# A drain after each piece of GpSimd's weight subtractions, in a two-block transformer kernel on one core

## The chip, the core and the metric

The kernel runs on one core of one Trainium2 chip. A core has five engines that take their own instruction streams and meet at semaphores: TensorE (PE in the rows, its weight loads PEld), VectorE (DVE), ScalarE (ACT), GpSimd (POOL) and SyncE (SP), which here issues the loads of weights. The metric is the device time of one execution in microseconds; the median of several runs is compared.

## The reference

Two transformer blocks follow each other on one sequence of 256 tokens with 1024 channels, all in float32.

```python
def reference(x, ...):
    x = first_block(x, ...)      # adaLN; retention + 3 groups of dilated attention, gated; squared-ReLU MLP (4096)
    return second_block(x, ...)  # 2 layers: MLA + mLSTM + SSD mixers, layernorm; hierarchical MoE, 16 experts of 256

proj = h @ w_in                                   # first block, 1024 x 12800
x = x + g2 * (jnp.square(jax.nn.relu(h @ w1)) @ w2)
h = jax.nn.silu(jnp.einsum('bsd,edf->bsef', x, w_gate)) * jnp.einsum('bsd,edf->bsef', x, w_up)
h = h * combine[..., None]                        # every expert is computed, weights are zero for most
return jnp.einsum('bsef,efd->bsd', h, w_down)
```

Nearly all of the time goes into products of the 256 tokens with weight matrices.

## The kernel before

The weights come as one stream of **units** of 128 partitions by 1024 columns, 448 of them through the engines in the same way (six rounds of eight more, for the modulation, go to VectorE alone). A float32 product is made of three products of rounded numbers: each operand is split into a high part (rounded, `_hi`) and the rest (`_lo`), and TensorE adds hi x hi, hi x lo and lo x hi (L923 to L925, helper `mm3`). A unit takes 12 matmuls of 512 columns: two token tiles, two halves, three products.

For each unit, in the order of the stream:

- SyncE loads two units at a time into `w_raw`, a ring of eight (L465). Before it overwrites a pair it waits for `lo_ready`.
- ScalarE writes the rounded copy into `w_hi`, a ring of four slots (L549, `hi`), once the data has landed and once TensorE has given the slot's former unit back (`unit_used`). It then increments `hi_ready`.
- GpSimd computes `w_lo = w_raw - w_hi` (L511, `lo`) once `hi_ready` has come, in pieces of `width` columns: two of 512 in the first block and for the experts, four of 256 in the front half of each layer of the second block. The last piece increments `lo_ready`.
- TensorE waits for `lo_ready`, multiplies, and increments `unit_used`.

The order is written out by hand, and each engine works through its list strictly. GpSimd does little else: 32 small products for the SSD mixer (L532) in each layer's middle and a few memsets. VectorE computes norms, rotations, softmax sums and the lo parts of the activations (L1505, L1513), multiplies the ada weights (L1583), squares the MLP's activations (L1846), weighs the experts' (L2209). It works on float32 and puts a `drain` between dependent operations of its own (`dep = dve.drain`).

The stages in order of the stream: retention inputs (units 0 to 47), first attention input, retention output, other attention inputs, gates, outputs (up to unit 127), the MLP (64 units, eight tiles), and then twice a layer of 128 units: inputs, MLA, mLSTM and SSD, output (31 units), router (1), experts (96, six for each).

Of the kernel before, what the change touches and what calls it, by code (L numbers as in the profile page):

```python
# [58 lines left out]
UNIT = 1024  # L59
# [116 lines left out]
def program(nc, A):  # L176

    ctx = ExitStack()
    with ctx:
# [272 lines left out]
        def spans(d):  # L452

            return ((0, 0, S), (1, P, S)) if d == 0 else ((0, 0, P), (1, 0, S))
# [7 lines left out]
        def _(sp):  # L462
# [15 lines left out]
            for (_, kind, k), (at, _, _) in zip(rounds, rounds[1:]):  # L478
                for s in range(n_ring):
                    used = k * RAW + PIECE * (s + 1)  # L480
                    sp.wait_ge(ada_used if kind == "ada" else lo_ready, used)
                    piece(at * n_ring + s, s)
                    if at == 1 and s == 1:
                        sp.dma_start(x_sb[:, :, :], A["x"].rearrange("b (t p) d -> p (b t) d", p=P)).then_inc(x_loaded, 16)
                        sp.dma_start(W[:, 0:D], A["norm1_g"].partition_broadcast(P)).then_inc(norm1_loaded, 16)
                if at == 1:
                    sp.dma_start(ident[:, :], A["identity"]).then_inc(ident_loaded, 16)
                if at == 2:
                    sp.dma_start(arena[:, 18432:20480], A["const1"]).then_inc(cst_loaded, 16)
                    sp.dma_start(inv_row, A["inv_freq"].partition_broadcast(P)).then_inc(pos_loaded, 16)  # L490
                    sp.dma_start(pos_i[:, :], A["pos_col"]).then_inc(pos_loaded, 16)
# [11 lines left out]
        @block.gpsimd  # L503
        def _(pool):
            pool.memset(mod[:, 2 * D:], 0.0).then_inc(mod_cleared_b, 1)
            def lo(n, k, width):

                pool.wait_ge(hi_ready, n + (k + 1))  # L508
                for a in range(0, UNIT, width):
                    cols = slice(a, a + width)  # L510
                    i = pool.tensor_tensor(w_lo[:, k % SLOTS, cols], w_raw[:, k % RAW, cols],  # L511
                                           w_hi[:, k % SLOTS, cols].bitcast(F32), ALU.subtract)
                i.then_inc(lo_ready, 1)

            def lo_round(n, width):
                for s in range(RAW):
                    lo(n, s, width)

            with pool.Fori(0, U_LAYERS // RAW) as i:
                lo_round(i * RAW, UNIT // 2)  # L520
            ahead = L_OUT + SLOTS
            with pool.Fori(0, LAYERS) as l:
                n = l * L_UNITS + U_LAYERS
                with pool.Fori(0, ahead // RAW) as i:
                    lo_round(i * RAW + n, UNIT // 4)
                for k in range(ahead // RAW * RAW, ahead):
                    lo(n, k, UNIT // 4)

                for j in range(2 * SH):
                    pool.wait_ge(sexp_ready, l * 8 + (j + 1))  # L530
                    for st, a, b in spans(j % 2):
                        i = pool.tensor_tensor(sw[:, j % 4, st, a:b], sw[:, j % 4, st, a:b], cbs[j // 4][:, st * S + a:st * S + b], ALU.mult)  # L532
                    i.then_inc(sw_ready, 1)
                for k in range(ahead, (ahead // RAW + 1) * RAW):
                    lo(n, k, UNIT // 4)
                with pool.Fori(ahead // RAW + 1, L_UNITS // RAW) as i:
                    lo_round(i * RAW + n, UNIT // 2)
# [1836 lines left out]
```

## Time and profile before

| | before |
|---|---|
| median of 3 runs | 1718.28 us (1718.05 to 1719.68) |
| the profiled execution's own time | 1714.52 us |
| its span in the trace | 1712.7 us, 20704 instructions |
| granted TensorE clock, mean | 0.941 |

The span is what the trace covers; the execution's own time lies 1.8 us above it. The profile is of one execution. Times in rows are microseconds from the span's start, or nanoseconds where it says so. Register, branch and drain instructions have no rows of their own in these views. A group of several instructions in the timeline ("x2") has the start of the first and the time to the end of the last.

### The profile page before, as it was taken

What the parts mean: (1) busy time and instruction counts of PE and PEld (TensorE: products, weight loads), DVE (VectorE), ACT (ScalarE), POOL (GpSimd) and SP (SyncE); (2) the same over time, 40 slices, a digit from 0 to 9 for tenths busy, and PEclk for the clock granted to TensorE, in tenths of its full rate; (3) what the DMA queues carried; (4) which work ended last, traced back from release to release, by engine and by line L of the source; (5) the groups of instructions that cost most, each with busy time, mean ns of one, the idle gap of its engine ahead of it and who ended that gap; (6) DMA issues with size and microseconds to landing.
All of it is one profiled execution on the core that took longest, in us unless ns stands there. A gap on an engine that the chain in (4) does not pass through costs nothing.

```text
span 1712.7 us, 20704 instructions
## 1 busy us (share of the span) xinstructions
PE 1516.0 (89%) x6848; PEld 1221.3 (71%) x6848; DVE 649.9 (38%) x1092; ACT 716.5 (42%) x1049; POOL 1231.9 (72%) x1061
## 2 busy tenths in 40 slices
PE   6979799999777999887787899999778778999996
PEld 2767577888665888676666688888667656888885
DVE  7666924222545111456745100010467463000003
ACT  4322444445433444344443444444344433444442
POOL 3887797877573999685226799999575355999994
PEclk8989999999897999998898899999889888999998
DMA  9665667444432555353103454555442023555551
GB/s 386 246 231 188 252 225 264 172 148 148 160 131 98 196 174 193 123 200 112 58 1 116 167 196 175 192 190 180 156 147 91 25 87 122 188 182 194 184 184 50
DMA packets 44043, 279.72 MB, mean 163 GB/s; under 512 B 5405, under 2 KB 8605, under 8 KB 11582
## 3 DMA queue, kind: packets, MB, share of 16 engines
q1 hardware_dynamic: 37138, 263.82, 42.7%
q10 hardware_dynamic: 6830, 14.92, 2.4%
q8 instruction: 44, 0.72, 0.2%
q14 instruction: 31, 0.25, 0.0%
HBM read 274.53 MB, written 4.19 MB: 163 GB/s over the span
## 4 chain that ended last, share of the span: by engine, by line
POOL 50%; issue 31%; PE 16%; DVE 1%; POOLq 1%; DVEq 0%; ACT 0%; ACTq 0%
POOL w_lo L511 49%; PE G L923 3%; PE G L924 3%; PE G L925 3%; PE AC L923 2%; PE AC L925 2%; PE AC L924 2%; POOL arena L532 1%; PE T L1006 0%; POOLq L508 0%; DVE x_sb L1858 0%; DVE x_sb L1856 0%; DVE sm L1915 0%; DVE x_sb L1878 0%; PE T L962 0%
## 5 line engine op out<-in xcount | busy, mean ns | idle before, releaser
L511 POOL TENSOR_TENSOR w_lo<-w_raw,w_hi 128x512 fp32r<-128x512 f32 (+1 forms) x1024 | 1210.4, 1211 | 446.4 <-ACT w_hi L549 446.2
L549 ACT ACTIVATE w_hi<-w_raw 128x1024 fp32r<-128x1024 f32 x448 | 471.9, 1059 | 641.2 <-PE G L925 355.9
L923 PE MATMUL G<-w_hi,xT_hi 128*128 128x512 f32 x944 | 391.4, 415 | 34.0 <-POOL w_lo L511 22.9
L924 PE MATMUL G<-w_lo,xT_hi 128*128 128x512 f32 x944 | 379.2, 402 | 0.0
L925 PE MATMUL G<-w_hi,xT_lo 128*128 128x512 f32 x944 | 378.6, 401 | 0.0
L923 PEld LDWEIGHTS G<-w_hi,xT_hi 128*128 128x128 f32 x944 | 185.2, 196 | 78.9 <-issue 19.8
L923 PE MATMUL AC<-w_hi,yT_hi 128*128 128x512 f32 x576 | 229.6, 399 | 6.6 <-DVE yT_lo L1505 4.4
L924 PE MATMUL AC<-w_lo,yT_hi 128*128 128x512 f32 x576 | 226.5, 393 | 0.0
L925 PE MATMUL AC<-w_hi,yT_lo 128*128 128x512 f32 x576 | 226.3, 393 | 0.0
L925 PEld LDWEIGHTS G<-w_hi,xT_lo 128*128 128x128 f32 x944 | 184.1, 195 | 40.9
L924 PEld LDWEIGHTS G<-w_lo,xT_hi 128*128 128x128 f32 x944 | 185.2, 196 | 36.0
L2209 DVE SCALAR_TENSOR_TENSOR arena<-arena,sm,G 128x256 f32<-128x256 f32 x64 | 27.9, 478 | 335.3 <-ACT arena L592 335.3
L1505 DVE TENSOR_TENSOR yT_lo<-T,yT_hi 128x256 fp32r<-128x256 f32 (+2 forms) x128 | 53.9, 458 | 247.1 <-ACT yT_hi L561 246.8
L923 PEld LDWEIGHTS AC<-w_hi,yT_hi 128*128 128x128 f32 x576 | 110.7, 192 | 31.1 <-POOL w_lo L511 3.7
L925 PEld LDWEIGHTS AC<-w_hi,yT_lo 128*128 128x128 f32 x576 | 110.0, 191 | 23.3
L924 PEld LDWEIGHTS AC<-w_lo,yT_hi 128*128 128x128 f32 x576 | 110.5, 192 | 22.1
L923 PE MATMUL AC<-w_hi,xT_hi 128*128 128x512 f32 x256 | 106.1, 415 | 6.1 <-POOL w_lo L511 5.9
L925 PE MATMUL AC<-w_hi,xT_lo 128*128 128x512 f32 x256 | 100.6, 393 | 0.0
L924 PE MATMUL AC<-w_lo,xT_hi 128*128 128x512 f32 x256 | 100.6, 393 | 0.0
L1006 PE MATMUL T<-ident,arena 128*128 128x128 f32 x292 | 49.0, 301 | 47.7 <-DVE arena L2209 13.7
L1583 DVE SCALAR_TENSOR_TENSOR mod<-w_raw,sm,mod 128x1024 f32<-128x1024 f32 x48 | 76.0, 1584 | 18.0 <-DMA w_raw<-w_stream 14.8
L1006 PEld LDWEIGHTS T<-ident,arena 128*128 128x128 f32 x292 | 38.2, 154 | 61.7 <-issue 42.4
(366 smaller groups left out, 1402.7 us busy)
## 6 DMA issues: line engine op xcount, KB each, us to landing
w_raw<-w_stream SPq DMA_DIRECT2D x248, 1024.0 KB, 4.8
mod<-rows ACTq DMA_DIRECT2D x2, 2048.0 KB, 10.1
rel_scratch<-arena ACTq DMA_DIRECT2D x1, 3072.0 KB, 18.1
mod<-rows ACTq DMA_DIRECT2D x3, 476.0 KB, 3.7
x_sb<-x SPq DMA_DIRECT2D x1, 1024.0 KB, 9.4
arena<-const SPq DMA_DIRECT2D x1, 1024.0 KB, 9.6
mod<-gn_g ACTq DMA_DIRECT2D x1, 1024.0 KB, 6.6
arena<-gn_b ACTq DMA_DIRECT2D x1, 1024.0 KB, 8.7
```

Of the source, the lines that this page charges most:

```text
L511: i = pool.tensor_tensor(w_lo[:, k % SLOTS, cols], w_raw[:, k % RAW, cols], w_hi[:, k % SLOTS, cols].bitcast(F32), ALU.subtract)
L532: i = pool.tensor_tensor(sw[:, j % 4, st, a:b], sw[:, j % 4, st, a:b], cbs[j // 4][:, st * S + a:st * S + b], ALU.mult)
L549: act.activation(w_hi[:, k % SLOTS, :], w_raw[:, k % RAW, :], ACT.Copy).then_inc(hi_ready, 1)
L923: pe.matmul(out, xh, wh, start=start, stop=False)
L924: pe.matmul(out, xh, wl, start=False, stop=False)
L925: return pe.matmul(out, xl, wh, start=False, stop=stop)
L1006: i = pe.transpose(T[:, t, c * P:(c + 1) * P], src[:, t, c * P:(c + 1) * P], ident[:, :])
L1505: dve.tensor_tensor(dst_lo[:, c0:c0 + nch, s], T[:, t, 0:nch * P].rearrange("p (c n) -> p c n", n=P), dst_hi[:, c0:c0 + nch, s].bitcast(F3 ...
L1583: dve.scalar_tensor_tensor(m, w_raw[:, s, :], csil[:, s:s + 1], m, ALU.mult, ALU.add).then_inc(ada_used, 1)
L2209: i = dve.scalar_tensor_tensor(moe_h[:, t, :], ffn_a[:, t, :], comb[:, bass.ds(e0 + (t * EXPERTS + e), 1)], G[:, t, DE:2 * DE], ALU.mult, ...
```

## The change

`lo` gets a drain of GpSimd behind each piece: between two pieces of a unit, and behind the last piece of each unit, whose increment of `lo_ready` stays on the piece itself. This holds in all stages, for both widths. A drain makes the engine's sequencer wait until what it has issued is complete before it issues more.

```diff
@@ def lo(n, k, width)
                     i = pool.tensor_tensor(w_lo[:, k % SLOTS, cols], w_raw[:, k % RAW, cols],
                                            w_hi[:, k % SLOTS, cols].bitcast(F32), ALU.subtract)
+                    if a + width < UNIT:
+                        pool.drain()
                 i.then_inc(lo_ready, 1)
+                pool.drain()
```

No other instruction moves. On GpSimd this is the end of the loop over the first block's units, before the change (`w_lo`, `w_raw` and `w_hi` as above; L519 is the loop, L508 the wait in `lo`):

```order
L508 REGISTER_ALU
L511 TENSOR_TENSOR w_lo<-w_raw,w_hi 128x512 [waits hi_ready]
L511 TENSOR_TENSOR w_lo<-w_raw,w_hi 128x512
L519 REGISTER_ALU
L519 COMPARE_AND_BRANCH
```

The register instruction computes the value that the next unit's wait needs; it stands behind the last piece, and at a loop's end a branch stands there too. After the change the rows are the same with a drain behind each piece, so that these instructions come after a drain.

## Rows read from the trace of the kernel before

**Rows 1.** The page: busy us, share of the span, instructions.
```profile
PE 1516.0 (89%) x6848; PEld 1221.3 (71%) x6848; DVE 649.9 (38%) x1092; ACT 716.5 (42%) x1049; POOL 1231.9 (72%) x1061
```
**Rows 2.** Windows: length; PE, PEld, DVE, ACT, POOL busy; clock, DMA, GB/s.
```profile
237.00:500.00 263.00, 246.56 (x1163) 201.08 (x1163) 92.37 (x150) 121.97 (x189) 193.65 (x151) 0.97 0.51 179
717.00:770.00 53.00, 43.74 (x186) 34.05 (x184) 31.94 (x46) 24.88 (x40) 44.13 (x58) 0.90 0.44 159
955.00:1211.00 256.00, 254.88 (x1153) 210.75 (x1152) 26.27 (x62) 110.27 (x134) 224.13 (x176) 1.00 0.52 185
```
**Rows 3.** Timeline, second layer's experts: start, us, instruction, idle before.
```profile
1504.45 0.87 DVE L2209 SCALAR_TENSOR_TENSOR arena<-arena,sm,G 128x256 f32<-128x256 f32 x2 [10.94 <-ACT arena L592]
...
1521.25 0.87 DVE L2209 SCALAR_TENSOR_TENSOR arena<-arena,sm,G 128x256 f32<-128x256 f32 x2 [10.93 <-ACT arena L592]
...
1600.86 1.06 ACT L549 ACTIVATE w_hi<-w_raw 128x1024 fp32r<-128x1024 f32 x1 [1.66 <-PE G L925]
...
1602.00 2.55 POOL L511 TENSOR_TENSOR w_lo<-w_raw,w_hi 128x512 fp32r<-128x512 f32 x2 [0.17 <-ACT w_hi L549]
...
1603.24 1.30 POOL L511 TENSOR_TENSOR w_lo<-w_raw,w_hi 128x512 fp32r<-128x512 f32 x1
1603.38 0.39 PE L923 MATMUL AC<-w_hi,yT_hi 128*128 128x512 f32 x1
...
1606.10 0.39 PE L923 MATMUL AC<-w_hi,yT_hi 128*128 128x512 f32 x1
...
1609.15 0.19 PEld L923 LDWEIGHTS G<-w_hi,xT_hi 128*128 128x128 f32 x1
```
**Rows 4.** Groups of instructions by line and form, GpSimd.
```profile
L511 POOL TENSOR_TENSOR w_lo<-w_raw,w_hi 128x512 fp32r<-128x512 f32 x768 | 1021.6, 1357 | 261.0 <-ACT w_hi L549 260.8
L511 POOL TENSOR_TENSOR w_lo<-w_raw,w_hi 128x256 fp32r<-128x256 f32 x256 | 188.8, 775 | 185.4 <-ACT w_hi L549 185.4
```
**Rows 5.** The page: a costly group (busy us, mean ns), DMA issues (KB, landing us).
```profile
L2209 DVE SCALAR_TENSOR_TENSOR arena<-arena,sm,G 128x256 f32<-128x256 f32 x64 | 27.9, 478 | 335.3 <-ACT arena L592 335.3
...
w_raw<-w_stream SPq DMA_DIRECT2D x248, 1024.0 KB, 4.8
```
**Rows 6.** One line's instructions: ns min/median/max, first and last start, forms.
```profile
L511 POOL TENSOR_TENSOR w_lo<-w_raw,w_hi x1024: 713/1288/2350, 32.8 to 1690.0; 128x512 fp32r<-128x512 f32 x128, 128x256 fp32r<-128x256 f32 x43
...
L1583 DVE SCALAR_TENSOR_TENSOR mod<-w_raw,sm,mod x48: 1270/1285/2148, 6.7 to 278.2; 128x1024 f32<-128x1024 f32 x48
```
**Rows 7.** Timeline, VectorE, group norm of a retention head.
```profile
193.98 1.23 DVE L1669 TENSOR_TENSOR arena<-arena 128x1024 f32<-128x1024 f32 x1
195.28 1.23 DVE L1674 TENSOR_TENSOR arena<-arena 128x1024 f32<-128x1024 f32 x1
```
**Rows 8.** Timeline, MLP, VectorE and GpSimd.
```profile
582.26 1.50 DVE L1846 TENSOR_TENSOR arena<-arena 128x1024 f32<-128x1024 f32 x1 [10.91 <-ACT arena L590]
...
604.95 1.50 DVE L1846 TENSOR_TENSOR arena<-arena 128x1024 f32<-128x1024 f32 x1 [10.94 <-ACT arena L590]
...
604.08 3.52 POOL L511 TENSOR_TENSOR w_lo<-w_raw,w_hi 128x512 fp32r<-128x512 f32 x2 [0.17 <-ACT w_hi L549]
```
**Rows 9.** Waits from 717 to 770, then from 115 to 240: us, times, longest.
```profile
PEld G L923 <- POOL w_lo L511: 5.8, 4, 2.8
...
PE G L923 <- POOL w_lo L511: 8.9, 2, 7.4
```
**Rows 10.** Timeline, GpSimd, chains at a layer's start and before 250 us.
```profile
740.29 11.38 POOL L511 TENSOR_TENSOR w_lo<-w_raw,w_hi 128x256 fp32r<-128x256 f32 x16 [5.46 <-ACT w_hi L549]
752.33 22.24 POOL L511 TENSOR_TENSOR w_lo<-w_raw,w_hi 128x256 fp32r<-128x256 f32 x32 [0.66 <-ACT w_hi L549]
...
898.49 16.89 POOL L511 TENSOR_TENSOR w_lo<-w_raw,w_hi 128x256 fp32r<-128x256 f32 x22 [21.55 <-ACT w_hi L549]
...
213.81 35.36 POOL L511 TENSOR_TENSOR w_lo<-w_raw,w_hi 128x512 fp32r<-128x512 f32 x25
```
**Rows 11.** Timeline, GpSimd, from 58 us.
```profile
59.45 18.28 POOL L511 TENSOR_TENSOR w_lo<-w_raw,w_hi 128x512 fp32r<-128x512 f32 x11
```

## The prediction, made before the changed kernel was run

> **What bounds the kernel now.** I read the busy shares first, then windows by stage, then the order in time of the steady stages. TensorE is busy 89% of the span, GpSimd 72%, ScalarE 42%, VectorE 38% [rows 1]. The windows show two kinds of stage [rows 2]. Among the experts TensorE is busy 254.88 of 256.00 us at granted clock 1.00, its upper level, 2.4 GHz. At the start of a layer it is busy only 43.74 of 53.00 us, at 0.90.
>
> The steady order is in [rows 3]. TensorE begins a unit every 2.72 us (1603.38, 1606.10, then 1609.15 after four transposes). ScalarE rounds a unit in 1.06 us, as soon as TensorE has given a slot back. GpSimd starts 0.08 us after that (1600.86 + 1.06 = 1601.92, start 1602.00), needs 2.55 us for its two pieces, and stands idle 0.17 us. So GpSimd is nearly as slow as TensorE here: its idle 28% of the span is not one reserve, and in the steady stages it comes in crumbs of 0.17 us.
>
> What protects TensorE is a **lead**. The unit whose subtraction ends at 1604.55 is first used at 1609.15, 4.6 us later; the one at 1606.10 was ready already. A stage can thus lose about 4.5 us on GpSimd before TensorE notices, once, unless TensorE pauses for something else and the lead grows back. Where the lead is gone already, each lost nanosecond counts: at the first layer's start its weight load waits 5.8 us for L511, and before 240 us TensorE waits 8.9 us for it [rows 9].
>
> **What one drain costs.** The program holds 448 units: 384 with 768 pieces of 512 columns and 64 with 256 pieces of 256 [rows 4]. The change adds a drain behind each of the 1024 pieces. Nothing is removed, no DMA is added. Queued behind a drain are, on GpSimd, the next piece, and at a unit's end the register instruction and the next wait for hi_ready. The increment of lo_ready sits on the last piece, ahead of its drain, so a drain inside a unit delays that unit, and the one at its end only the next. Behind these wait TensorE (lo_ready) and SyncE, whose loads wait for lo_ready too; a load refills a slot needed eight units later (over 21 us) and lands in 4.8 us [rows 5], so that stays covered as long as that distance holds.
>
> The trace shows no drained GpSimd piece, so I bound it. Undrained, the second piece starts 1.24 us after the first (1602.00, 1603.24), whose kind lasts 1.288 us in the median [rows 3, 6]: they overlap by 0.05 us. A drain removes this overlap at least: 0.05 us is the lower bound. A GpSimd piece released by another engine's completion starts 0.08 us after it, as above; 0.05 + 0.08 = 0.13 us. VectorE has drains in this kernel: L1667, L1669 and L1674 have one between each two, and L1669 (193.98 + 1.23) is followed by L1674 at 195.28, 0.07 us later; two undrained L2209 take 0.87 us against 2 x 0.478, so they overlap by 0.09; the difference is 0.16 us [rows 5, 7]. I take **0.14 us**, between the two ways of reading it. At a unit's end the register instruction, which now runs while the piece is being computed, comes after the drain. No row shows its time. It is bounded by nothing and by the 0.08 us in which a whole wait is answered; I take 0.04. The register and branch instructions at a loop's end, once in eight units, are a few more of the kind: 0 to 0.6, I take 0.3, or 0.04 a unit.
>
> A unit of two pieces then costs 0.14 + 0.18 + 0.04 = **0.36 us** more, and a back-to-back unit goes from 2.50 (2.55 less the 0.05) to 2.86 us. A unit of four pieces costs 3 x 0.14 + 0.18 + 0.02 = **0.62 us** more.
>
> The Trainium skill (GPSIMD Engine Reference, section 3.1) puts the dispatch of one VectorE instruction at about 156 ns and says that GpSimd has two software hops where VectorE has one. An estimate from that page, 2 x 156 = 0.31 us a drain, would about double what I take, and the sum with it; the start after 0.08 us in this trace speaks against it.
>
> **Where it lands on the path.**
> - *Experts.* One expert is six units in 16.80 us (L2209 at 1504.45 and 1521.25 [rows 3]). Drained, GpSimd needs 6 x 2.86 = 17.16, so 0.36 too much; 16 experts make 5.8, less the lead of 4.5: 1.3 us a layer, **2.6 us**.
> - *MLP.* A tile of eight units takes 22.69 us (L1846 at 582.26 and 604.95); one piece of a tile is held up by that VectorE operation (3.52 against 2.55 us) [rows 3, 8]. Drained: 8 x 2.86 + 0.97, less 0.14 since the held-up piece was going to wait anyway, is 23.7: 1.0 too much, seven times, less at most 4.5 of lead. Between 2.5 and 7, I take **5 us**.
> - *Layer starts.* Here the units have four pieces, and GpSimd runs them without a gap: 16 pieces from 740.29, 32 in 22.24 us from 752.33 (2.78 a unit), 22 from 898.49 [rows 10], that is some 17 units a layer, with TensorE waiting for them [rows 9]. Some of them still fill slots before TensorE needs them; I count 13 of the 17: 13 x 0.62 = 8 us a layer, **16 us**. This is the largest term.
> - *First 300 us.* Again chains without a gap (25 pieces from 213.81 [rows 10]). Until about 240 us many pieces alternate with VectorE's operations of two inputs (11 pieces in 18.28 us, 1.66 each instead of 1.25 [rows 11]). A piece that stands waiting for VectorE loses nothing by starting 0.14 us later. I count the free ones: some 20 units x 0.36 = **7 us**.
> - *Attention inputs and gates, and the rest of each layer.* From 237 to 500 us GpSimd is busy 193.65 of 263.00 us [rows 2]: idle for a quarter, and with the lead that covers 0.36 us in each unit of some 3.5: nothing. Without that cover the 60-odd units there would cost 0.36 each, 22 us.
>
> Sum: 2.6 + 5 + 16 + 7 = 30.6 us. Made against the profiled execution (span 1712.7, its time 1714.52) that is 1745.1 us. The median of the runs is 1718.28, 3.8 us above the profiled one, so I forecast 1718.3 + 30.6, **1749 us**.
>
> Ends: with 0.05 us a drain and nothing for registers, a unit of two costs 0.10 and one of four 0.20. MLP and experts stay under TensorE's time (8 x 2.60 + 0.97 = 21.8), and 26 x 0.20 + 20 x 0.10 = 7 us remain: 1725. With 0.16 a drain and 0.13 for registers at every unit's end, a unit of two costs 0.45, of four 0.77. MLP: 8 x 2.95 + 0.8 = 24.4, 1.7 x 7 - 4.5 = 7; experts 2 x (16 x 0.9 - 4.5) = 20; layer starts 26 x 0.77 = 20; first stretch 9; together 56: 1774.
>
> **Rivals.**
> 1. *No change:* the drain ends with the piece, and the 0.17 us of idle take in all that is left. For it: those gaps. Against it: the chains without a gap, with TensorE waiting behind them; it needs a drain under 0.02 us, below the overlap that is surely lost. Time 1718.
> 2. *Faster, by the port that GpSimd and VectorE share.* Operations of VectorE are held up by L511's pieces: L1583, 48 times before 280 us, lasts 1285 ns in the median and up to 2148 [rows 6]. If the pause after each piece lets such operations through, each gains up to 0.86 us; with half of the 48 held up that is 20 us at most. At my price of a drain it does not pay for the 30.6; with the drain at 0.05 (7 us) it decides from 9 such waits on, and all 24 gone give 1718 + 7 - 20 = 1705. Against it: in the alternating stretch the two engines already take turns after every single piece [rows 11], and a pause of 0.1 us in 1.4 meets an operation 1 time in 14, under 2 us in all. The Trainium skill (SBUF — State Buffer, "SBUF: two separate sides") calls the shared pair an exclusive lock that is held for the whole instruction; the trace agrees, with waits of 0.86 us.
> 3. *A dear drain.* A unit takes 2.78 us in four pieces and 2.50 in two [rows 3, 10], so each piece has a fixed part of 0.14 us. If a queued piece hides most of a larger one, and an emptied engine shows it again, a drain costs 0.13 + 0.14 = 0.27 us, with registers 0.6 a unit of two (3.1 us) and 1.14 a unit of four: MLP 8 x 3.1 + 0.9 = 25.7, 3 x 7 - 4.5 = 16; experts 2 x (16 x 1.8 - 4.5) = 49; layer starts 26 x 1.14 = 30; first 12: 107 us, 1825. For it: a drain has to empty the engine, which no row shows. Against it: both nearest gaps are 0.07 and 0.08.
>
> **Chances.** Forecast, a drain of 0.05 to 0.17 us: 0.78. No change: 0.05. Faster: 0.04. Dear: 0.13. The range runs from 1720 to 1780: it takes in my two ends and reaches down into the no-change case, and leaves out the faster and the dear one. A measurement of this kernel can tell about 0.2%, 3.4 us. Faster 0.04, same 0.05, slower 0.91.
>
> **What the profile after should show.** In the experts GpSimd's two pieces taking 2.70 to 2.75 us instead of 2.55 and lying 2.82 to 2.88 us apart, its waits for L549 gone there late in the stage, TensorE waiting for L511 in small steps, an expert lasting 17.0 to 17.2 us near its end. At the layers' starts a unit of four pieces in 3.4 instead of 2.79 us. VectorE's and ScalarE's own durations as before. The prediction is wrong if the pieces themselves get longer, if the clock shows more stretches at its lower level, 1.2 GHz, because TensorE pauses (from 717 to 770 us the clock is 0.90 with TensorE busy 83% of the time; from 237 to 500 it is 0.97 at 94% [rows 2]), or if VectorE's held-up operations become fewer.

## The result and the profile after

The changed kernel takes 1794.51 us in the median, the kernel before 1718.16 in the same comparison: 1.0455 of it, 95% interval 1.0428 to 1.0482. The forecast of slower was right, but 1749 was not, and 1794.5 lies above the range: 76 us were added where 30.6 were predicted. The profiled execution took 1793.63 us, span 1791.8. Medians here and below are of executions that agree: one of the four of E2 took 3806 us and is left out of its median.

The page of the changed kernel: a group (busy us, mean ns, idle before it and what ended it), then the chain that ended last.

```profile
POOLq 68%; issue 27%; PE 3%; POOL 1%; DVE 0%; DVEq 0%; ACT 0%
...
L511 POOL TENSOR_TENSOR w_lo<-w_raw,w_hi 128x512 fp32r<-128x512 f32 (+1 forms) x1024 | 1227.1, 1198 | 501.5 <-ACT w_hi L552 327.4
```

The pieces are no longer than before (mean 1198 ns; the page of before has 1211). The time went into the gaps behind them: the chain that ended last runs now through GpSimd's queue (POOLq, 68%, nearly all of it at the two drains' lines, L514 and L516); in the page of before it had GpSimd's pieces for 50% and TensorE for 16%. In the waits of GpSimd, 92.5 us in 365 places wait for nothing that the profile shows:

```profile
POOL w_lo L511 <- ACT w_hi L552: 327.4, 85, 28.5
POOL w_lo L511 <- issue: 92.5, 365, 0.6
```

Timeline of the changed kernel among the second layer's experts, the place of [rows 3]:

```profile
1642.48 0.87 DVE L2212 SCALAR_TENSOR_TENSOR arena<-arena,sm,G 128x256 f32<-128x256 f32 x2 [11.67 <-ACT arena L595]
...
1660.17 0.87 DVE L2212 SCALAR_TENSOR_TENSOR arena<-arena,sm,G 128x256 f32<-128x256 f32 x2 [11.37 <-ACT arena L595]
...
1678.17 0.87 DVE L2212 SCALAR_TENSOR_TENSOR arena<-arena,sm,G 128x256 f32<-128x256 f32 x2 [11.37 <-ACT arena L595]
...
1649.70 2.73 POOL L511 TENSOR_TENSOR w_lo<-w_raw,w_hi 128x512 fp32r<-128x512 f32 x2 [0.22 <-issue]
1652.48 0.19 PEld L926 LDWEIGHTS G<-w_hi,xT_hi 128*128 128x128 f32 x1 [0.33 <-POOL w_lo L511]
1652.65 2.73 POOL L511 TENSOR_TENSOR w_lo<-w_raw,w_hi 128x512 fp32r<-128x512 f32 x2 [0.22 <-issue]
1655.42 0.19 PEld L926 LDWEIGHTS G<-w_hi,xT_hi 128*128 128x128 f32 x1 [0.36 <-POOL w_lo L511]
1655.90 2.73 POOL L511 TENSOR_TENSOR w_lo<-w_raw,w_hi 128x512 fp32r<-128x512 f32 x2 [0.53 <-issue]
```

The reader sees all the prices here. Two pieces take 2.73 us instead of 2.55: the second now starts 0.14 us after the first one's end instead of 0.04 to 0.05 before it, so the drain between them costs about 0.19. Behind a unit there are 0.22 us of gap instead of an overlap of 0.04, so the second drain with the register instruction costs 0.26, and a loop's end has a gap of 0.53, 0.31 more. Units lie 2.95 us apart. TensorE waits for L511 in both units that the rows show, and an expert takes 18.00 us (1660.17 to 1678.17) instead of 16.80. At a layer's start, the place of [rows 10]:

```profile
759.92 3.37 POOL L511 TENSOR_TENSOR w_lo<-w_raw,w_hi 128x256 fp32r<-128x256 f32 x4 [4.66 <-ACT w_hi L552]
763.51 3.35 POOL L511 TENSOR_TENSOR w_lo<-w_raw,w_hi 128x256 fp32r<-128x256 f32 x4 [0.22 <-issue]
```

A unit of four pieces takes 3.59 us instead of 2.78, 0.81 more. In the MLP, the place of [rows 8], a tile takes 24.58 us instead of 22.69:

```profile
636.75 2.13 DVE L1849 TENSOR_TENSOR arena<-arena 128x1024 f32<-128x1024 f32 x1 [10.93 <-ACT arena L593]
...
661.33 2.12 DVE L1849 TENSOR_TENSOR arena<-arena 128x1024 f32<-128x1024 f32 x1 [10.97 <-ACT arena L593]
```

**Stage by stage.** TensorE executes the same 6848 weight loads in each of the kernels here, so the start of the same load in two traces compares them place by place. The table gives the length of a stretch in the profiled execution of the kernel before, and what each kernel adds to it; in brackets the microseconds in which the clock was granted at its lower level, 1.2 GHz.

| stretch of before, us | length | after | E1 mid | E2 end | E3 wide | E4 narrow |
|---|---|---|---|---|---|---|
| 7 to 272, first stretch | 265.6 (34) | +10.1 (34) | +1.1 (34) | +8.4 (20) | +10.2 (34) | +1.5 (17) |
| 272 to 564 | 291.1 (38) | -3.0 (34) | -1.9 (34) | -2.6 (34) | -2.7 (34) | 0.0 (38) |
| 564 to 722, MLP | 158.2 (0) | +10.6 (4) | 0.0 (0) | +1.8 (0) | +10.8 (4) | 0.0 (0) |
| 722 to 857, layer 1 | 134.9 (38) | +4.9 (40) | +3.5 (38) | +0.7 (38) | -4.8 (26) | +2.5 (27) |
| 857 to 898, SSD and mLSTM | 41.9 (7) | +10.4 (34) | +10.1 (31) | +10.2 (34) | +1.6 (14) | +10.7 (34) |
| 898 to 962 | 63.1 (20) | +2.9 (20) | +3.3 (20) | +0.5 (14) | -2.5 (14) | +1.1 (14) |
| 962 to 1220, experts | 258.4 (6) | +11.8 (4) | 0.0 (6) | 0.0 (3) | +12.9 (5) | 0.0 (3) |
| 1220 to 1239, layer 2 starts | 19.2 (4) | +3.8 (3) | +4.1 (8) | +2.2 (7) | 0.0 (5) | +5.3 (11) |
| 1239 to 1341, layer 2 | 102.1 (17) | +3.2 (19) | +5.9 (27) | +0.4 (17) | +0.7 (17) | +6.6 (27) |
| 1341 to 1377, SSD and mLSTM | 35.8 (7) | +9.4 (29) | +10.4 (31) | +10.0 (31) | +0.1 (7) | +10.9 (31) |
| 1377 to 1445 | 67.6 (20) | +2.5 (20) | +3.4 (27) | +3.2 (27) | -0.4 (20) | +3.7 (24) |
| 1445 to 1700, experts | 255.0 (0) | +11.9 (0) | 0.0 (0) | 0.0 (0) | +13.0 (0) | 0.0 (0) |

Two stretches stand out that the prediction had at nothing: the SSD and mLSTM part of each layer, 10.4 and 9.4 us, each with over 20 us more at the lower clock. GpSimd has almost no weights to subtract there (one unit of four pieces; the other 16 of its 20 instructions in the rows below are products for the SSD mixer). Windows over this part, of the kernel before and then of the changed one (length; PE, PEld, DVE, ACT, POOL busy; clock, DMA, GB/s):

```profile
857.00:898.00 41.00, 33.23 (x196) 27.77 (x196) 20.26 (x49) 17.58 (x45) 12.15 (x20) 0.92 0.00 1
```
```profile
880.00:931.00 51.00, 45.45 (x196) 38.85 (x195) 19.81 (x47) 16.96 (x45) 12.07 (x20) 0.67 0.00 1
```

The same 196 matmuls, at clock 0.67 instead of 0.92, take 45.45 us of TensorE instead of 33.23.

The short stretch from 1220 to 1239 is the start of the second layer. Weight loads wait there for GpSimd's pieces, in the kernel before (1220 to 1240) and in the changed one (1268 to 1292):

```profile
PEld G L923 <- POOL w_lo L511: 5.8, 3, 3.4
```
```profile
PEld G L926 <- POOL w_lo L511: 10.2, 4, 4.1
```

### The profile page after: what moved, and what is told of

It is laid out like the page before. It is cut to its first block, busy times and chain, and to the rows that moved or that the text cites. A ratio compares the mean times of both kernels' runs of the same rounds, so it can differ in the third digit from the quotient of the medians.

```text
span 1791.8 us, 21728 instructions
## 1 busy us (share of the span) xinstructions
PE 1577.8 (88%) x6848; PEld 1235.8 (69%) x6848; DVE 637.4 (36%) x1092; ACT 716.6 (40%) x1049; POOL 1248.6 (70%) x1061
## 4 chain that ended last, share of the span: by engine, by line
POOLq 68%; issue 27%; PE 3%; POOL 1%; DVE 0%; DVEq 0%; ACT 0%
POOLq L514 36%; POOLq L516 31%; POOL arena L535 1%; POOLq L508 1%; PE AC L926 1%; PE AC L927 0%; PE G L926 0%; PE AC L928 0%; PE G L928 0%; PE G L927 0%; POOLq L539 0%; POOL w_lo L511 0%; POOLq L522 0%; DVE x_sb L1859 0%; DVEq L1536 0%
## 5 line engine op out<-in xcount | busy, mean ns | idle before, releaser
L511 POOL TENSOR_TENSOR w_lo<-w_raw,w_hi 128x512 fp32r<-128x512 f32 (+1 forms) x1024 | 1227.1, 1198 | 501.5 <-ACT w_hi L552 327.4
L926 PE MATMUL G<-w_hi,xT_hi 128*128 128x512 f32 x944 | 396.0, 420 | 45.6 <-POOL w_lo L511 32.4
L926 PE MATMUL AC<-w_hi,yT_hi 128*128 128x512 f32 x576 | 240.0, 417 | 20.7 <-POOL w_lo L511 16.3
L926 PE MATMUL AC<-w_hi,xT_hi 128*128 128x512 f32 x256 | 108.2, 422 | 10.9 <-POOL w_lo L511 10.8
L1586 DVE SCALAR_TENSOR_TENSOR mod<-w_raw,sm,mod 128x1024 f32<-128x1024 f32 x48 | 79.8, 1662 | 20.8 <-DMA w_raw<-w_stream 17.5
L1009 PE MATMUL T<-ident,arena 128*128 128x128 f32 x292 | 49.2, 302 | 42.1 <-DVE arena L2212 11.8
## 6 DMA issues: line engine op xcount, KB each, us to landing
mod<-rows ACTq DMA_DIRECT2D x2, 2048.0 KB, 10.1
```

What stands on the lines that cost most here:

```text
L926: pe.matmul(out, xh, wh, start=start, stop=False)
L1009: i = pe.transpose(T[:, t, c * P:(c + 1) * P], src[:, t, c * P:(c + 1) * P], ident[:, :])
L1586: dve.scalar_tensor_tensor(m, w_raw[:, s, :], csil[:, s:s + 1], m, ALU.mult, ALU.add).then_inc(ada_used, 1)
```

## The experiments

### Which of the two drains, and in which units

E1, drains between the pieces only:

```diff
                     if a + width < UNIT:
                         pool.drain()
                 i.then_inc(lo_ready, 1)
-                pool.drain()
```


> Only the drains between the pieces of a unit (576 of the 1024); none behind the last piece. The trace of the changed kernel shows the next piece 0.14 us after a drained one's end instead of 0.04 before it: 0.19 us each. Theory A (a pipeline with a lead: a unit's time counts only where GpSimd becomes slower than TensorE or the lead is gone): a unit of two pieces takes 2.69 us, under TensorE's 2.80 among the experts and 2.84 in the MLP, so both stages cost nothing; the layers' starts (0.56 a unit) and the first 300 us cost 20 us, 1738. Rival B (each drain costs its share of the 76 us wherever it stands, 75 ns each): 43 us, 1761. If the clock's longer lower stretch in the mLSTM and SSD part comes back with these drains, 20 us more on A: 1758, and the windows there tell it.

E2, the drain behind the unit only:

```diff
-                    if a + width < UNIT:
-                        pool.drain()
                 i.then_inc(lo_ready, 1)
                 pool.drain()
```


> Only the drain behind the last piece of each unit (448 of the 1024). The trace of the changed kernel shows the next unit 0.22 us after the last piece's end instead of 0.04 before: 0.27 us each, 0.57 at a loop's end. Theory A: a unit of two pieces takes 2.77 us and one in eight 3.08, 2.81 in the mean: about TensorE's pace, so MLP and experts cost under 5 us; all together 15 us, 1733. Rival B (75 ns a drain): 33 us, 1751. A and this run's sum with the one without end drains would give 35 of 76 us: the rest arises only when both stand together. With the clock's part 20 us more.

E3, both, in units of two pieces only (E4 the same with `UNIT // 4`):

```diff
-                    if a + width < UNIT:
+                    if a + width < UNIT and width == UNIT // 2:
                         pool.drain()
                 i.then_inc(lo_ready, 1)
-                pool.drain()
+                if width == UNIT // 2:
+                    pool.drain()
```


> Both kinds of drain, but only in units of two pieces of 512 columns (first block, MLP, experts); the layers' starts as before. Theory A with the measured prices: first 300 us 10, MLP 12, experts 2 x 12, together 47 us, 1765, and the mLSTM and SSD part without a longer stretch at the lower clock. Rival B: 768 drains of 75 ns, 57 us, 1775.

> Both kinds of drain, but only in units of four pieces of 256 columns (the front of each layer of the second block). Theory A: 10 to 12 us a layer while TensorE waits for GpSimd at the layer's start and at the output projection, 24 us, 1742; and if the long stretch at the lower clock in the mLSTM and SSD part is set off by these delays, 20 us more, 1762. Rival B: 256 drains of 75 ns, 19 us, 1737, with the clock as before. With the run of the wide units alone the two sums should add up to 76 us: theory A says the stages are independent.

| | median, us | ratio, 95% interval |
|---|---|---|
| kernel before (with E1 to E4) | 1719.5 | |
| E1, 576 drains | 1754.3 | 1.0184, 1.0124 to 1.0245 |
| E2, 448 drains (three executions) | 1745.24 | 1.0140, 1.0064 to 1.0215 |
| E3, 768 drains | 1756.3 | 1.0210, 1.0150 to 1.0269 |
| E4, 256 drains | 1755.87 | 1.0199, 1.0140 to 1.0258 |

The medians alone decide nothing: E1 lies between theory A's 1738 and its 1758 with the clock, E2 between A's 1733 and the 1751 of 75 ns a drain, to which A with the clock's part (1753) comes close. The stretches decide. In the MLP and the experts of the two layers E1 adds 0.0, 0.0 and 0.0, E2 1.8, 0.0 and 0.0, both together (E3) 10.8, 12.9 and 13.0. A price per drain cannot give that: the 256 drains of either kind there would have to cost the same alone as together. The timelines show why. GpSimd among the experts, first E1, then E2:

```profile
1499.20 2.73 POOL L511 TENSOR_TENSOR w_lo<-w_raw,w_hi 128x512 fp32r<-128x512 f32 x2
1502.39 16.35 POOL L511 TENSOR_TENSOR w_lo<-w_raw,w_hi 128x512 fp32r<-128x512 f32 x12 [0.47 <-ACT w_hi L551]
1519.21 1.28 POOL L511 TENSOR_TENSOR w_lo<-w_raw,w_hi 128x512 fp32r<-128x512 f32 x1 [0.47 <-ACT w_hi L551]
```
```profile
1559.28 2.55 POOL L511 TENSOR_TENSOR w_lo<-w_raw,w_hi 128x512 fp32r<-128x512 f32 x2 [0.22 <-issue]
1562.05 2.55 POOL L511 TENSOR_TENSOR w_lo<-w_raw,w_hi 128x512 fp32r<-128x512 f32 x2 [0.22 <-issue]
1564.91 2.55 POOL L511 TENSOR_TENSOR w_lo<-w_raw,w_hi 128x512 fp32r<-128x512 f32 x2 [0.31 <-issue]
1567.67 2.54 POOL L511 TENSOR_TENSOR w_lo<-w_raw,w_hi 128x512 fp32r<-128x512 f32 x2 [0.22 <-issue]
1570.84 2.54 POOL L511 TENSOR_TENSOR w_lo<-w_raw,w_hi 128x512 fp32r<-128x512 f32 x2 [0.62 <-issue]
```

E1 runs six units in 16.35 us and then still waits 0.47 us for ScalarE: six fit into an expert's 16.80. E2 uses 2.77 us for most units and 22.6 us for eight with the loop's end, where TensorE needs 22.4: over the 96 units that is some 2.4 us, and the lead of 4.6 takes it in. Both together need 3.00 us a unit with the loop's end. So E3 gives theory A its 10.8 in the MLP (12 expected) and 13 us a layer in the experts (12), and 1756.3 instead of 1765 since the stretches at 272 to 564 and 722 to 857 gave back 7.5 us, most of it with less time at the lower clock.

The other half: in all runs with drains in the narrow units (E1, E2, E4) the SSD and mLSTM part takes 10 to 11 us more a layer, with 31 or 34 us at the lower clock; in E3 it takes 1.6 and 0.1. E4's 1755.87 comes nearer to the 1762 that was expected with the clock's part than to the 1742 without it or to the 1737 of 75 ns a drain. E3 and E4 add up to 37 + 36 = 73 of the 76 us.

### What sends the clock down

In each layer GpSimd's program has three units (12 pieces) right before the products for the SSD mixer, on which TensorE waits. E5 drains these three alone; E6 is the changed kernel without these; E7 has no drain, but the last of the three in eight pieces of 128 columns.

```diff
 # E5 (E6: the reverse); drained is an argument of lo() that guards both drains
                 for k in range(ahead // RAW * RAW, ahead):
-                    lo(n, k, UNIT // 4)
+                    lo(n, k, UNIT // 4, True)
```


> Drains, of both kinds, only in the three units of each layer that stand right before the SSD products on GpSimd (12 drains a layer, 24 in all); everything else as before. In the runs with drains in the layers' front the stretch from the first of these products to the end of that part took 10 to 11 us longer a layer, beside 20 us more at the lower clock, and it did not where only the wide units had drains. Theory C: a delay of well under 1 us on GpSimd's way to the products makes TensorE's pause fall so that the clock goes to its lower level for some 27 us instead of 3: this kernel then takes 2 x 10 us more for 24 drains, 1738. Rival D: it takes the sum of delays from the whole front of a layer: then this kernel is at 1719 to 1721 and shows the clock as before. At 75 ns a drain it would be 2 us.

> The changed kernel without the drains in those three units of each layer, 1000 of the 1024 drains. Theory C: the long stretch at the lower clock goes, and with it 20 us: 1775. Rival D: 1793, as the changed kernel.

```diff
 # E7, from the kernel before
                 for k in range(ahead // RAW * RAW, ahead):
-                    lo(n, k, UNIT // 4)
+                    lo(n, k, UNIT // 8 if k == ahead - 1 else UNIT // 4)
```


> The kernel before, without any drain, but the last unit before the SSD products is subtracted in eight pieces of 128 columns instead of four of 256. A piece has a fixed part of about 0.14 us, so the unit ends 0.5 to 0.6 us later, like a unit with drains. Theory C: if it is the delay and not the drain that sends the clock down, this kernel shows the same 10 us a layer, 1738. Rival E, that a drain does something of its own there: 1719 with the clock as before.

| | median, us | ratio, 95% interval | SSD and mLSTM part, two layers, us added |
|---|---|---|---|
| kernel before (with E5 to E8) | 1717.92 | | |
| E5, 24 drains | 1738.52 | 1.0104, 1.0043 to 1.0165 | 12.0, 9.2 |
| E6, 1000 drains | 1782.77 | 1.0360, 1.0298 to 1.0422 | 9.8, 8.6 |
| E7, no drain | 1734.29 | 1.0089, 1.0064 to 1.0114 | 10.3, 9.4 |

By the medians 24 drains cost 20.6 us, a quarter of what 1024 do, and a kernel without any drain, whose last unit merely ends later, costs 16.4. The kernel before scatters in this comparison (1713.8 to 1733.75), which makes the intervals wide; both lie above 1. GpSimd before the products, in the kernel before and in E7:

```profile
858.59 3.26 POOL L511 TENSOR_TENSOR w_lo<-w_raw,w_hi 128x256 fp32r<-128x256 f32 x4 [20.01 <-ACT w_hi L549]
861.81 4.45 POOL L532 TENSOR_TENSOR arena<-arena,scr 128x256 f32<-128x256 f32 x8
```
```profile
859.99 3.82 POOL L511 TENSOR_TENSOR w_lo<-w_raw,w_hi 128x128 fp32r<-128x128 f32 x8 [20.13 <-ACT w_hi L549]
863.78 4.42 POOL L532 TENSOR_TENSOR arena<-arena,scr 128x256 f32<-128x256 f32 x8
```

and the windows over the part in E7:

```profile
857.00:909.00 52.00, 44.87 (x198) 38.57 (x199) 19.64 (x47) 17.59 (x47) 12.68 (x24) 0.70 0.00 1
```

The unit takes 3.82 instead of 3.26 us, 0.56 longer, and the clock is 0.70, near the 0.67 after the change. It is thus the delay, not the drain (against rival E), and a delay of 0.6 us is enough (against rival D). In the kernel before, the clock stays at its upper level for 27 us from 852 on and then falls for 3.4 us (6.8 in the second layer). In both layers of the changed kernel and of E1, E2, E4, E5 and E7 it falls after 13.7 us and stays down for 27 to 31 us; in E3 it stays up for 27 us as before. Windows in the first layer, one of before and two of the changed kernel:

```profile
852.00:879.50 27.50, 25.13 (x177) 21.71 (x175) 9.12 (x27) 14.09 (x40) 12.15 (x20) 0.99 0.01 1
```
```profile
875.00:889.00 14.00, 12.30 (x76) 9.88 (x75) 6.76 (x19) 7.93 (x21) 6.55 (x11) 0.98 0.00 1
889.50:920.00 30.50, 30.00 (x118) 26.80 (x119) 5.84 (x18) 11.03 (x27) 5.02 (x9) 0.50 0.00 1
```

TensorE had pauses before it fell (12.30 us busy of 14.00), and by the profile, which models the matmuls' ends, hardly any while the clock stayed down (30.00 of 30.50). Which of the pauses decides, and why the clock does not come back sooner, no run here shows. The kernel before can take the slower course too, it seems: one of its 13 executions in this comparison took 1733.75 us at a mean clock of 0.925, where the other twelve have 0.933 to 0.946. It has no trace. E6 speaks against the narrow form of theory C: its profiled execution, at 1793.73, has both long stretches although the three units are undrained, while its other four runs took 1779.98 to 1782.94 us, at mean clocks of 0.935 to 0.937 against 0.929. So these units are enough to set it off but not the only ones that can, and the time differs from run to run. That the four faster runs lack one of the two stretches fits their 11 us, but no trace of theirs shows it, and the mean clock does not tell it surely: two executions of the changed kernel at 1794.5 us have 0.932 and 0.935.

### The price of one more drain

E8, every drain twice:

```diff
                     if a + width < UNIT:
                         pool.drain()
+                        pool.drain()
                 i.then_inc(lo_ready, 1)
                 pool.drain()
+                pool.drain()
```


> Each of the 1024 drains twice. The second finds an idle engine, so it costs only what the sequencer needs for one more such instruction: between the end of a drain and the start of the next instruction the trace of the changed kernel has 0.07 us, so about 0.08 us each. Theory A (a lead that is already used up, so all of it counts in the stages where GpSimd sets the pace): a tile of the MLP 16 x 0.08 = 1.3 us, an expert 12 x 0.08 = 1.0, the layers' starts 26 x 0.32 = 8, the first 300 us 3: together 9 + 31 + 8 + 3 = 51 us over the changed kernel, 1845. If a drain's price were the emptying of the engine alone, the second would be free: 1794.

1840.68 us, 1.0701 (1.0637 to 1.0765): 46 us over the changed kernel, 51 expected, where a free second drain would have left it at 1794. GpSimd among the experts:

```profile
1769.11 1.29 POOL L511 TENSOR_TENSOR w_lo<-w_raw,w_hi 128x512 fp32r<-128x512 f32 x1 [0.21 <-issue]
1770.69 1.29 POOL L511 TENSOR_TENSOR w_lo<-w_raw,w_hi 128x512 fp32r<-128x512 f32 x1 [0.29 <-issue]
1772.19 1.29 POOL L511 TENSOR_TENSOR w_lo<-w_raw,w_hi 128x512 fp32r<-128x512 f32 x1 [0.21 <-issue]
```

The gaps are 0.21 and 0.29 us where the changed kernel has 0.14 and 0.22: 0.07 for a second drain, which has nothing to wait for. It is not free, so a drain's price is not the emptying alone. The drains' own records, which these views leave out, divide the 0.19 us of a first drain in the changed kernel: 0.05 is the overlap that is lost, 0.05 passes from the piece's end to the drain's, and 0.09 from there to the next piece's start (medians of 574 places).

### Making room under the threshold, and wider pieces

E9 is the changed kernel with the wide units in one piece, E10 the same without drains (the edit for the first block and the MLP; the experts have the same):

```diff
-                lo_round(i * RAW, UNIT // 2)
+                lo_round(i * RAW, UNIT)
```


> The changed kernel, but the units of the first block, the MLP and the experts are subtracted in one piece of 1024 columns instead of two of 512, so that a wide unit has one drain, behind it. A piece's fixed part is 0.14 us: a unit takes 2.36 + 0.27 + 0.04 = 2.67 us, under the 2.80 of TensorE among the experts and the 2.84 in the MLP. Theory A (threshold): MLP and experts are back at the times of the kernel before in spite of a drain in every unit; what is left is the layers' fronts with their clock stretch (the run with the narrow units alone: 36 us) and 3 us before 300 us: 1757. Rival B (a drain costs 75 ns wherever it stands): 448 - 64 + 256 = 640 drains, 48 us, 1766. Rival F: a piece twice as long holds up VectorE's operations longer (up to 2.4 us instead of 1.2): another 5 to 10 us in the first 300 us and in the MLP.

> No drains; the wide units in one piece of 1024 columns. Where GpSimd sets the pace (chains without a gap in the first 300 us) 0.14 us a unit are saved, 3 us; elsewhere TensorE sets it: 1715. Rival F, the longer hold on VectorE, would put it at 1720 to 1730.

E9 takes 1775.86 us (1.0362, 1.0329 to 1.0394), not 1757; E10 1743.57 (1.0150, 1.0121 to 1.0180), not 1715. As a total E9 is nearer to the 1766 of 75 ns a drain; the stretches separate the two questions. Against the kernel before, E9 adds 0.0 us in the MLP and 0.0 in the experts of either layer: with a drain behind each of the 256 units, nothing. GpSimd there:

```profile
1563.16 2.41 POOL L511 TENSOR_TENSOR w_lo<-w_raw,w_hi 128x1024 fp32r<-128x1024 f32 x1 [0.33 <-ACT w_hi L552]
1565.88 2.39 POOL L511 TENSOR_TENSOR w_lo<-w_raw,w_hi 128x1024 fp32r<-128x1024 f32 x1 [0.31 <-ACT w_hi L552]
```

2.39 us and a gap of 0.22 fit under 2.72, and it waits for ScalarE again. That is theory A at its plainest. In the first 272 us E9 and E10 lose 16.4 and 12.8 us, more than rival F said; E9 also has 58 us at the lower clock there, against 34 in the kernel before and 31 in E10. VectorE in E10, in a rotation:

```profile
63.85 2.89 DVE L1631 TENSOR_TENSOR arena<-arena 128x512 f32<-128x512 f32 x1
66.81 2.74 DVE L1633 TENSOR_TENSOR arena<-arena 128x512 f32<-128x512 f32 x1
69.47 2.89 DVE L1634 TENSOR_TENSOR arena<-arena 128x512 f32<-128x512 f32 x1
```

GpSimd does eight pieces in 21.47 us around them, 2.68 each, so the two engines take turns. The same operations last 1.62 to 1.78 us in the kernel before, beside pieces half as long, and 0.68 to 0.69 where nothing holds them up. E10 has a long clock stretch in the second layer besides (8.9 us added), without a drain and with the last unit hardly longer (3.38 us against 3.26), so a shift of another origin can set it off too.

E11 and E12 go the other way in the layers' fronts, without drains: E11 takes two pieces of 512 instead of four of 256 in all the units there, E12 only in the three before the SSD products.

```diff
 # E12; E11 has the same edit in the other two places of the front
                 for k in range(ahead // RAW * RAW, ahead):
-                    lo(n, k, UNIT // 4)
+                    lo(n, k, UNIT // 2)
```


> No drains; the units in the front of each layer in two pieces of 512 instead of four of 256. 0.28 us less a unit on some 13 units a layer for which TensorE waits: 7 us saved, 1711. Rival F: VectorE's small operations there wait up to 1.2 us instead of 0.7 for each piece: slower, 1720 to 1730. The clock's stretch after the SSD products need not change, since the units before them end earlier, not later.

> No drains; only the three units right before the SSD products in two pieces of 512. They end up to 0.8 us earlier. Theory C says that these units' end decides over the clock's long stretch: earlier is safe, so 1717 to 1718, and none of the runs at 1724 to 1734 that the kernel before shows now and then. If the clock depends on the place of the pause in both directions, it may as well show the long stretch: 1738.

E11 takes 1712.78 us against 1717.39 of before: 0.9980, 0.9965 to 0.9994, faster by a little than the kernel before, where 1711 was expected. It saves 7.0 us from 722 to 857, and gives part back in the second layer. E12 takes 1721.84, 1.0020 (1.0004 to 1.0036), neither the 1717 to 1718 nor the 1738 expected. Its last unit before the products takes 2.96 us instead of 3.26. No stretch of 27 us at the lower clock appears, but an earlier end is not free either: there are 17 us at the lower level in the first layer's SSD part instead of 7, which adds 2.8 us, and 30 instead of 17 from 1239 to 1341, which adds 4.7.

## Why the prediction was wrong

- **The mechanism behind the four terms of the sum was right.** GpSimd stops hiding behind TensorE where it becomes slower than it, or where the lead is gone. E1, E2, E3 and E9 show the threshold from both sides. The changed kernel's experts and MLP tiles, at 18.00 and 24.58 us, are what the units give: 6 x 2.95 + 0.31 for the loop's end, and 8 x 2.95 + 0.31 + 0.69 for the piece that the VectorE operation holds up.
- **The step that failed first is the price of a drain.** I took 0.14 us and 0.18 at a unit's end with the registers, "between the two ways of reading it". Measured: 0.19 and 0.26. The start 0.08 us after another engine's completion, on which the 0.13 rested, is not the start behind a drain: that comes 0.14 us after the piece's end, and E8 puts 0.07 us on one more drain alone. VectorE's 0.16 was nearer. A unit of two so costs 0.19 + 0.26 + 0.04 = 0.49 us instead of 0.36, a third more than I took. Since the cost counts above a threshold, the terms grew by far more: an expert has 1.2 us over TensorE's time instead of 0.36, so the experts' 2.6 us became 23.7 (11.8 and 11.9 a layer), and the MLP's 5 became 10.6.
- **The step that failed second is "the rest of each layer: nothing".** 19.8 us came from the SSD and mLSTM parts, where the products begin some 0.6 us later a layer by the drains themselves (3.61 + 0.23 us from the last unit's start, instead of 3.26 less an overlap of 0.04), and nearly all of the rest goes with the lower clock. The prediction named the clock as something that would make it wrong, in the wrong place: it looked for it where TensorE would wait for L511, and it came in a part whose pauses are there anyway, after a delay of 0.6 us.
- **Layers' starts, 16 us, came out near, by luck in part:** 17.3 us in the five stretches around them. The price was too low and the count too high: at 0.81 us instead of 0.62, 17.3 us are 21 units in both layers instead of 26.
- **First 300 us:** 7 forecast, 10.1 less 3.0 in the next stretch measured. The count of 20 free units at the new price of 0.49 gives 9.8, near the 10.1. No run confirms the count: E1 adds 1.1 there and E2 8.4 at another share of lower clock.
- **Rivals.** No change and faster are excluded. VectorE's held-up operations did not become fewer: L1583, now L1586, has a mean of 1662 ns instead of 1584, and the squaring in the MLP takes 2.13 us instead of 1.50. The dear drain, given 0.13, was 0.27 us with 1825 us as its sum. The measured price lies between the two: a unit of two costs 0.49 us, against my 0.36 and the 0.60 of this rival, and the experts 23.7 against my 2.6 and its 49. In total the rival was off by 31 us and I by 46. The estimate of 0.31 us a drain from the Trainium skill (GPSIMD Engine Reference, section 3.1) was too high by the trace's 0.19 and 0.26. At that price the sum would not have doubled either, as I wrote, but more than tripled: the rival with 0.27 us a drain comes to 107. But it pointed the right way, and my reason for setting it aside, the start after 0.08 us, did not hold.
- **The upper end, 1774, was too low because it held nothing for the clock.** Its prices, 0.45 and 0.77 us a unit, are close to the measured 0.49 and 0.81, and its sum of 56 us is close to what is left of the 78.5 us in the table without the SSD and mLSTM parts' 19.8: 58.7. Without that second step the time would have fallen inside the range, at about 1777, though far from the forecast.
- **What the profile should show.** Two pieces in 2.73 us came as forecast (2.70 to 2.75), and so did four, in 3.35 to 3.37 (3.4). Units lie 2.95 us apart, not 2.82 to 2.88: the gap behind a unit was the worse guess.

## What to carry to other kernels

Where TensorE set the pace, a drain on a helper engine cost nothing here until that engine's time for one round, with everything in its loop, passed the bounding engine's; then all that was above counted. So first compute the room (here 2.80 - 2.51 = 0.29 us a unit), and where it is small against the possible prices, give the term a wide range: 0.49 instead of 0.36 us a unit made 2.6 us into 23.7. Two additions that are each free can be dear together. And in a part where TensorE pauses often, look at the granted clock when a time does not add up: a delay of 0.6 us moved 10 us here.

## What the runs showed of the hardware that was not expected

- A drain on GpSimd between two pieces costs 0.19 us, at a unit's end with a register instruction 0.26, a second one behind it 0.07.
- A subtraction of 512 columns takes 1.25 us back to back and one of 256 0.70; one of 1024 takes 2.39. From these, an estimate of the fixed part of each is 0.11 to 0.15 us.
- In a part with many matmuls and pauses (33.23 us busy of 41) the clock stayed at 1.2 GHz for 27 to 31 us in some kernels, with TensorE busy for 30.00 of 30.50 us, and 3 to 10 in others. The long stretch cost some 10 us each time, and a unit that ended 0.6 us later was enough for it.
- A VectorE operation of two inputs of 512 columns that meets GpSimd's stream lasts 0.3 to 0.5 us longer than GpSimd's piece: 1.62 to 1.78 us beside pieces of 512 columns, 2.7 to 2.9 beside 1024, instead of 0.68 to 0.69.
